# Latent attention: the product of high rope keys by low queries on 64 rows of the array instead of 128

## What is computed

```python
s = (jnp.einsum('bqhd,bkhd->bhqk', qn, k_nope, preferred_element_type=jnp.float32)
     + jnp.einsum('bqhd,bkd->bhqk', qp, k_pe, preferred_element_type=jnp.float32)) * scale
mask = k_chunk[None, :] <= (qpos // CHUNK)[:, None]
p = jax.nn.softmax(jnp.where(mask, s, -jnp.inf), axis=-1)
return jnp.einsum('bhqk,bkhd->bqhd', p.astype(v.dtype), v)
```

## Time and profile before

| | |
|---|---|
| median of three runs | 2582.79 us |
| profiled execution, span from first to last instruction | 2579.7 us |
| mean granted clock of TensorE | 0.998 |
| PE busy, PEld busy | 2526.1 us (98%), 2449.2 us (95%) |
| DVE, ACT, POOL busy | 1639.3 us, 1053.0 us, 806.2 us |
| stage of attention (first to last L2785) | 1552.7 to 1838.8 us |

### The profile page before, as it was taken

One profiled execution on the slowest core, in us unless ns is written; L12 is line 12 of the kernel. 1 busy time (PEld: TensorE's weight loads), 2 busy tenths in 40 slices (PEclk: granted clock), 3 DMA queues, 4 the chain that ended last, 5 costly groups with the idle time before them and its releaser, 6 DMA issues.

```text
span 2579.7 us, 44368 instructions
## 1 busy us (share of the span) xinstructions
PE 2526.1 (98%) x18550; PEld 2449.2 (95%) x18550; DVE 1639.3 (64%) x2626; ACT 1053.0 (41%) x1733; POOL 806.2 (31%) x532
## 2 busy tenths in 40 slices
PE   8999999999999999999999999999999999999999
PEld 6999999999999999999998998999999999999999
DVE  6735353569766665874724886666697666748754
ACT  6433333364333323332446676445453223333312
POOL 5131313162444444002522124223334444441002
PEclk9999999999999999999999999999999999999999
DMA  3111111132333234552113435132123333337522
GB/s 112 36 37 36 37 36 38 36 105 60 118 105 108 92 117 156 176 169 84 55 41 113 143 141 185 59 101 75 63 72 100 109 100 109 111 110 239 167 71 90
DMA packets 229682, 252.26 MB, mean 98 GB/s; under 512 B 16849, under 2 KB 178271, under 8 KB 228591
## 3 DMA queue, kind: packets, MB, share of 16 engines
q1 hardware_dynamic: 227087, 247.36, 29.1%
q10 hardware_dynamic: 2400, 2.10, 0.3%
HBM read 173.54 MB, written 75.89 MB: 97 GB/s over the span
## 4 chain that ended last, share of the span: by engine, by line
PE 79%; DVE 14%; issue 3%; ACT 2%; DMA 1%; SPq 0%; POOL 0%; DVEq 0%; ACTq 0%; POOLq 0%
PE ps L903 13%; PE ps L905 13%; PE ps L904 13%; PE ps L346 9%; PE ps L348 8%; PE ps L347 8%; PE ps L2816 3%; PE ps L1713 1%; PE ps L2801 1%; PE ps L1700 1%; PE ps L1701 1%; PE ps L1702 1%; DVE xT L1430 1%; DVE hflat L491 1%; PE ps L1789 1%
## 5 line engine op out<-in xcount | busy, mean ns | idle before, releaser
L1578 POOL TENSOR_TENSOR wlo<-wraw,whi 128x1024 fp32r<-128x1024 f32 x78 | 192.5, 2468 | 440.1 <-DVE s_raw L1265 440.1
L311 POOL TENSOR_TENSOR wlo<-wraw,whi 128x2048 fp32r<-128x2048 f32 (+1 forms) x21 | 94.3, 4492 | 565.1 <-ACT whi L304 535.5
L903 PE MATMUL ps<-hh,whi 128*128 128x264 f32 x928 | 264.6, 285 | 5.7 <-DVE wlo L1306 3.4
L904 PE MATMUL ps<-hl,whi 128*128 128x264 f32 x928 | 263.9, 284 | 0.0
L905 PE MATMUL ps<-hh,wlo 128*128 128x264 f32 x928 | 263.9, 284 | 0.0
L346 PE MATMUL ps<-hh,whi 128*128 128x352 f32 x648 | 218.5, 337 | 0.6 <-ACT cqr L3151 0.3
L590 DVE TENSOR_TENSOR xT<-xT,ps 128x352 f32<-128x352 f32 x288 | 147.4, 518 | 98.2 <-PE ps L348 97.7
L348 PE MATMUL ps<-hh,wlo 128*128 128x352 f32 x648 | 208.4, 322 | 0.0
L347 PE MATMUL ps<-hl,whi 128*128 128x352 f32 x648 | 208.0, 321 | 0.0
L903 PEld LDWEIGHTS ps<-hh,whi 128*128 128x128 f32 x928 | 174.7, 188 | 7.0 <-DVE wlo L1306 4.2
L1578 POOL TENSOR_TENSOR s_lo<-s_raw,s_hi 128x512 fp32r<-128x512 f32 x80 | 157.7, 1972 | 60.1 <-DVE wlo L1306 30.1
(11 more groups left out here) (462 smaller groups left out, 8677.8 us busy)
## 6 DMA issues: line engine op xcount, KB each, us to landing
wraw<-w_ffn_in SPq DMA_DIRECT2D x88, 512.0 KB, 3.8
s_a<-hf SPq DMA_DIRECT2D x44, 528.0 KB, 3.3
wraw<-w_ffn_out SPq DMA_DIRECT2D x44, 512.0 KB, 3.7
s_t<-h SPq DMA_DIRECT2D x16, 1056.0 KB, 4.5
hflat<-s_t SPq DMA_DIRECT2D x16, 1056.0 KB, 6.2
h<-s_a SPq DMA_DIRECT2D x12, 1056.0 KB, 5.5
wraw<-w_gla_in SPq DMA_DIRECT2D x24, 512.0 KB, 4.6
s_x<-xT SPq DMA_DIRECT2D x6, 1408.0 KB, 5.5
```

Source lines behind the costliest of these rows:

```text
L311: pool.tensor_tensor(lo[:, 0:cols], raw[:, 0:cols], hi[:, 0:cols].bitcast(F32), ALU.subtract).then_inc(S("w_lo"), 1)
L903: nc.tensor.matmul(out, w_[0], x_[0], start=first, stop=False, skip_group_check=True)
L904: nc.tensor.matmul(out, w_[0], x_[1], start=False, stop=False, skip_group_check=True)
L1578: return pool.tensor_tensor(lo[:, cols], raw[:, cols], hi[:, cols].bitcast(F32), ALU.subtract)
```

## The change

For a step with chunks c = 0, 1 the four products L346, L347, L348 and L2784 are made for all chunks first. Then low queries by high keys follows for each chunk, with 64 rows: chunk 0 takes rows 0 to 63 of `apl` and `kph`, chunk 1 takes rows 64 to 127. Both hold the same values there, so `kph` is not zeroed any more, and the wait before the attention counts to 4 instead of 5. A step with one chunk has one product of 64 rows.

```diff
                     pe.matmul(out, aph[sl][:, qs_], khl[:, keys], start=False, stop=False)
-                    last = pe.matmul(out, apl[sl][:, qs_], kph[:, keys], start=False, stop=True)
+                for c, (i, n) in enumerate(chunks(nk)):
+                    out = flat[0:m, score_col(s) + i:score_col(s) + i + n]
+                    rows, keys = slice(c * ROPE, (c + 1) * ROPE), slice(k0 + i, k0 + i + n)
+                    last = pe.matmul(out, apl[sl][rows, q0:q0 + m], kph[rows, keys], start=False, stop=True)
                 last.then_inc(S("scores"), 1)
...
-            pe.wait_ge(S("latent_lo"), 5)
+            pe.wait_ge(S("latent_lo"), 4)
             pe_att(pe)
...
-            dve.wait_ge(S("latent_lo"), 4)
-            dve.tensor_tensor(kph[low, :], kph[low, :].bitcast(F32), kph[low, :].bitcast(F32), ALU.subtract)\
-               .then_inc(S("latent_lo"), 1)
```

## The result

The changed kernel took 2595.7 us (median of four runs, 2594.73 to 2597.26) against 2582.89 us (2581.96 to 2583.36): +12.8 us, a ratio of 1.0050 with a 95% interval of 1.0035 to 1.0064. The profiled execution has a span of 2593.4 us, 13.7 us more than before. The forecast was 2599.0 us in a range of 2592 to 2605.

The account below looks back on a forecast made before the run. The prediction took PE as the bound in the attention. Row changes less the pairs' saving add 22.9 us, waits absorb 6.7: +16.2 on 2582.8 gives 2599.0 us, range 2592 to 2605.

Parts of the forecast that it names:

- What bounds it: In the attention PE is full, so a nanosecond on PE is one of the kernel's, except where PE waits.
- the two named kinds of wait: In the attention: fills behind short scores waiting for DVE's addition, 3.6 us absorbed; transposes waiting for probabilities, 3.1 us.
- The price of an excursion, 0.39 us: On PE, each step's going from 128 rows to 64 and back costs 0.39 us, 0.20 on each side.
- (d): At the row changes around L2788: only the 0.09 gap is paid, 0.18 us per excursion; 2587.0 us, chance 0.09.
- (e): At the row changes around L2788: height costs fp32r nothing; 2579.4 us, chance 0.07.
- The pair: In the 40 two-chunk steps, the second product's load comes 0.11 us after the first's; saves 3.4 us.
- rival (b): In the two-chunk steps: full overlap, the loads don't queue, 5.6 us saved; 2596.9 us, chance 0.12.
- Rival (a): In the two-chunk steps: no overlap of the pair, the 3.4 us saving is gone; 2602.2 us, chance 0.24.
- (c): Within a pair: going from lower to upper half drains too, 40 times 0.20 us; 2610 us, chance 0.05.
- What waits absorb, 6.7 us: Existing PE waits in the attention, for DVE's addition and for probabilities, take back 6.7 us of the added time.
- The sum: Whole kernel: 22.9 added less 6.7 absorbed gives +16.2 us, 2599.0 us, 0.6% slower; chance 0.43.
- DVE's edit: Removing the 1.79 us zeroing on DVE is worth nothing, since DVE waits 20.28 us for PE behind it.

Follow-up runs that it names:

- e3_singles: The changed kernel with 64 rows only in the 32 one-chunk steps; two-chunk steps use 128 rows, kph not zeroed: 2590.52 us, ratio 1.0030.
- e5_apart: The changed kernel with each chunk's 64-row product directly behind its own four, so no pairs: 2617.3 us, ratio 1.0132.
- e4_lower: The changed kernel with the second chunk's product on rows 0 to 63 as well: 2603.38 us, ratio 1.0079.
- e1_order: The changed kernel's order, but every product on all 128 rows and kph zeroed as in the kernel before: 2583.01 us, ratio 1.0001.
- e7_nozero: The kernel before without the zeroing of the upper rows of kph: 2583.93 us, ratio 1.0000.

## Why the prediction held, and where it was off

**What bounds it.** Right. PE was full, and what was added on PE came out as time, except where the two named kinds of wait stood.

**The price of an excursion, 0.39 us.** Right, from one place in the trace of before and for another data type, line and width. The prediction calls all products of 64 rows before the change two-pass ones; the nine transposes at L3088 are single ones, and their loads stall as well (in a group with two, 0.53 us more than with whole rows), so two passes are not what the cost comes with. Measured 0.37 to 0.40 in single steps of three kernels (the changed one, e3_singles, e5_apart). The reading that decided it was that both the gap of 0.09 us and the load behind it, 0.11, are paid on each side. Rivals (d) and (e) fall with that: the gap alone would have made 0.18, and e5_apart shows twice 0.39 in a step.

**The pair.** This is the term that was mis-sized, and the one place where the mechanism was wrong. I put the second load 0.11 us behind the first and so took 3.4 us of saving, where rival (b) had 5.6. The loads of different rows start together (3 to 4 ns apart); the queue of 0.11 exists, but for the same rows (e4_lower). In steps it is 0.16 instead of 0.27 for 1024 keys, 0.21 instead of 0.27, and 0.25 instead of 0.35. Rival (b), which had a chance of 0.12, gave 2596.9 us, 1.2 above the median; the forecast, with 0.43, was 3.3 above it. That the measured time lies in the range all the same is owed to the range, which was made to hold (b) too, and not to this term. The rule of rival (b), the Trainium skill's in "TensorE: Matmul & The Clock Gate", "Part 3: Packing small matmuls", is borne out: about 4 ns there, 3 to 4 ns in the trace. Rival (a) falls with it, and (c), the change of halves, too: the two don't wait for each other at all.

**What waits absorb, 6.7 us.** Right in kind: the steps of 128 keys lose nothing, those of 256 lose 0.10. In heads 2 and 3 the means are within a hundredth of what the arithmetic on the earlier trace rows gave; single steps of 256 keys lie between 0.08 and 0.13. In heads 0 and 1 the stage grew by 1.4 us (56.4 against 55.0 of e1_order), where the forecast, 5.7 less 3.1 for the probabilities, had 2.6, and full overlap 5.2 less 3.1, 2.1. So there the waits took some 0.7 us more than I had counted; this is a difference of sums, and which waits they are stays open.

**The sum.** Over e1_order the three later pairs of heads grew by 4.0 to 4.2 us each, 12.2 in all with the last exit, and the first pair by 1.4, in all 13.6. With the overlap in full the forecast's own arithmetic has +14.1. The median says 12.8 with an interval of 9 to 16.5, so the last microsecond is beyond what was measured. One stretch at half clock costs less here than the 1.7 us that the prediction gave it: heads 0 and 1 take 55.9 us in the kernel before, with one in them, and 55.0 in e7_nozero, which has the same attention without one. The half-clock stretches changed places between executions (in the attention before, at 1381 us after), and e1_order has one at 1380 us without any 64-row product in the attention, so no case rests on them.

**DVE's edit.** Nothing, as forecast (e7_nozero). What it had not foreseen on DVE is the slower multiplication in three steps, some 0.5 us.

## What to carry to other kernels

Before giving a product fewer rows, look at what stands on both sides of it in PE's queue: a lone product of 64 rows between products of 128 costs 0.39 us here, more than the product of 512 columns itself (0.23), while 80 or 96 rows cost nothing. One pair doesn't carry a going and a coming. By these prices two pairs of 512 columns between products of 128 rows would save 0.46 and cost 0.39; that is an estimate, and no kernel with several pairs together was run. And where operands are held twice or can be padded with zeros, the full height was the cheaper one (5.3 us here), save where it made outputs wider.

## What the runs showed that I had not expected

Loads of weights in different rows start together: 0.19 us for two, against 0.29 us when both go to the same rows. And a multiplication on DVE of 128 by 512 elements took from 0.49 to 1.25 us, by when the piece of GpSimd's subtraction under way at its start ended: 0.28 us behind that end, and never under 0.49. So a shift of 0.4 us on PE made a step 0.37 us longer in which nothing had changed.
